# Sums of squares of four RMS norms: eight TensorE products, or three VectorE halvings and one product

## The reference, cut to what is computed

```python
def rms_norm(x, g):
    xf = x.astype(jnp.float32)
    inv = lax.rsqrt(jnp.mean(xf * xf, axis=-1, keepdims=True) + EPS)
    return (xf * inv).astype(x.dtype) * g
...
def modulate(h, shift, scale):
    return h * (1 + scale[:, None, :]) + shift[:, None, :]
...
def ffn_sublayer(x, mod, base, g, w1, w3, w2):
    h = modulate(rms_norm(x, g), mod[:, base], mod[:, base + 1])
    gate = 1 + mod[:, base + 2][:, None, :]
    return x + MACARON_W * gate * swiglu(h, w1, w3, w2)
```

## Time and profile before

| what | us |
|---|---|
| median of 3 runs | 3716.43 |
| lowest and highest run | 3714.55, 3716.44 |
| span of the profiled execution (first to last instruction) | 3719.7 |
| PE busy | 3549.7 |
| DVE busy | 1276.8 |
| ACT busy | 909.3 |
| POOL busy | 705.8 |

### The profile page before, as it was taken

One profiled execution on the slowest core, in us unless ns is written; L12 is line 12 of the kernel. 1 busy time (PEld: TensorE's weight loads), 2 busy tenths in 40 slices (PEclk: granted clock), 3 DMA queues, 4 the chain that ended last, 5 costly groups with the idle time before them and its releaser, 6 DMA issues.

```text
span 3719.7 us, 53696 instructions
## 1 busy us (share of the span) xinstructions
PE 3549.7 (95%) x21007; PEld 3244.3 (87%) x21007; DVE 1276.8 (34%) x2798; ACT 909.3 (24%) x1360; POOL 705.8 (19%) x282
## 2 busy tenths in 40 slices
PE   8889999999999999999998998888999999999997
PEld 2269999999988999999998888444998999999997
DVE  1242322223256232232413766333324232223225
ACT  0031111111134232322323665222013111111112
POOL 0012322232201111111122221000111322223220
PEclk9999999999999999999999999999999999999999
DMA  8721111111111313131443333887510111111101
GB/s 303 240 76 34 45 40 50 34 42 37 57 51 61 106 65 106 48 117 54 151 146 109 89 92 82 276 279 254 194 56 28 35 44 56 34 34 45 50 18 51
DMA packets 245498, 343.11 MB, mean 92 GB/s; under 512 B 56093, under 2 KB 164053, under 8 KB 245138
## 3 DMA queue, kind: packets, MB, share of 16 engines
q1 hardware_dynamic: 218962, 308.42, 25.9%
q10 hardware_dynamic: 26432, 33.18, 2.4%
HBM read 293.54 MB, written 48.01 MB: 92 GB/s over the span
## 4 chain that ended last, share of the span: by engine, by line
PE 89%; DVE 3%; DMA 3%; issue 2%; ACT 2%; SPq 2%; DVEq 0%; ACTq 0%
PE psum L269 24%; PE psum L273 24%; PE psum L272 24%; PE psum L465 4%; PE psum L1412 3%; DMA kn<-k_t 2%; PE psum L1642 2%; PE psum L1392 1%; PE psum L1629 1%; PE psum L990 1%; DVE h_f L612 1%; PE psum L1379 1%; PE psum L1673 1%; PE psum L594 1%; SPq L1596 1%
## 5 line engine op out<-in xcount | busy, mean ns | idle before, releaser
L269 PE MATMUL psum<-acts_hi,w_hi 128*128 128x384 f32 x4032 | 1372.1, 340 | 29.4 <-issue 18.5
L273 PE MATMUL psum<-acts_hi,w_lo 128*128 128x384 f32 x4032 | 1359.8, 337 | 0.0
L272 PE MATMUL psum<-acts_lo,w_hi 128*128 128x384 f32 x4032 | 1359.8, 337 | 0.0
L259 POOL TENSOR_TENSOR w_lo<-w_raw,w_hi 128x2048 fp32r<-128x2048 f32 x106 | 494.1, 4670 | 1821.4 <-ACT w_hi L253 1821.4
L269 PEld LDWEIGHTS psum<-acts_hi,w_hi 128*128 128x128 f32 x4032 | 761.9, 189 | 35.6 <-issue 30.8
L272 PEld LDWEIGHTS psum<-acts_lo,w_hi 128*128 128x128 f32 x4032 | 761.8, 189 | 3.3
L273 PEld LDWEIGHTS psum<-acts_hi,w_lo 128*128 128x128 f32 x4032 | 761.5, 189 | 0.0
L806 DVE TENSOR_TENSOR u_f<-psum,gated 128x384 f32<-128x384 f32 x132 | 73.6, 558 | 994.2 <-ACT gated L761 994.2
L829 DVE SCALAR_TENSOR_TENSOR x<-psum,mods,x 128x384 f32<-128x384 f32 (+1 forms) x552 | 314.9, 570 | 194.6 <-PE psum L273 194.6
L253 ACT ACTIVATE w_hi<-w_raw 128x2048 fp32r<-128x2048 f32 x106 | 200.5, 1910 | 644.4 <-PE psum L269 606.0
L269 PE MATMUL psum<-u_hi,w_hi 128*128 128x384 f32 x1056 | 357.6, 339 | 0.0
(11 more groups left out here) (224 smaller groups left out, 2880.5 us busy)
## 6 DMA issues: line engine op xcount, KB each, us to landing
w_raw<-in_ffn_w SPq DMA_DIRECT2D x66, 1024.0 KB, 5.4
ada_w<-in_w_ada SPq DMA_DIRECT2D x18, 2048.0 KB, 9.6
kc<-in_cache_k SPq DMA_DIRECT2D x16, 2048.0 KB, 10.3
vc<-in_cache_v SPq DMA_DIRECT2D x16, 2048.0 KB, 8.5
w_raw<-in_w_in SPq DMA_DIRECT2D x28, 1024.0 KB, 5.2
sp<-sample_bias SPq DMA_DIRECT2D x128, 65.0 KB, 6.7
ada_w<-in_w_ada_f SPq DMA_DIRECT2D x4, 2048.0 KB, 15.6
kf<-k_t SPq DMA_DIRECT2D x32, 256.0 KB, 4.6
```

The costliest lines, as they stand in the source:

```text
L259: eng.tensor_tensor(w_lo[st][:], w_raw[raw][:], w_hi[st][:].bitcast(F32), ALU.subtract).then_inc(sem("w_lo_done"), 1)
L269: pass1 = eng.matmul(out, whi, ahi, start=first, stop=False)
L272: eng.matmul(out, whi, alo, start=False, stop=False)
L273: return eng.matmul(out, wlo, ahi, start=False, stop=last)
```

## The change

Between the square and the sum stands a new step, `norm_fold`: DVE adds the upper half of the channel blocks of `sq` to the lower half, in place, three times (8 blocks to 4, to 2, to 1), each addition waiting for the one before. `norm_sum` is then one product of the block that is left. The folds are placed by hand in DVE's order: norm 0 all three ahead of `norm_inverse` 0; norms 1 and 3 in the last pass of the FFN, chunk c-1 after the addition of block 3 of chunk c, and chunk 2 after the last addition; norm 2 after the additions of q = 20, q = 22 and q = 23. The last pass of `ffn_vector` is written out. The new semaphore `sq_folded` takes the place of `lf16_turned` and `new_f_ready`, whose increments go to `state_rows_turned` and `lf16_moved`.

```diff
+    FOLDS = 3
+
+    def norm_fold(eng, n, c):
+
+        g = NC * n + c
+        s = sq[:, :, tokens_of(c)]
+        eng.wait_ge(sem("sq_ready"), g + 1)
+        for step in range(FOLDS):
+            half = KT // 2 >> step
+            if step:
+                eng.wait_ge(sem("sq_folded"), FOLDS * g + step)
+            eng.tensor_tensor(s[:, 0:half, :], s[:, 0:half, :], s[:, half:2 * half, :], ALU.add).then_inc(sem("sq_folded"), 1)
+
     def norm_sum(eng, n, c):
 
-        eng.wait_ge(sem("sq_ready"), NC * n + c + 1)
-        for k in range(KT):
-            last = eng.matmul(stats(n, c), ones[:], sq[:, k, tokens_of(c)], start=(k == 0), stop=(k == KT - 1))
-        last.then_inc(sem("ss_ready"), 1)
+        eng.wait_ge(sem("sq_folded"), FOLDS * (NC * n + c + 1))
+        eng.matmul(stats(n, c), ones[:], sq[:, 0, tokens_of(c)], start=True, stop=True).then_inc(sem("ss_ready"), 1)
...
     def norm_vector(eng, n):
+        if n == 0:
+            for c in range(NC):
+                norm_fold(eng, n, c)
         norm_inverse(eng, n, 0)
...
-        def body(i, first_step):
+        def body(i, first_step, last_step=False):
...
                     add_gated(eng, ps[4 + d % 4], x, d, c, gate, "y_free", it * 8 + d + f * KT)
+                    if last_step and c >= 1 and d == 3:
+                        norm_fold(eng, 2 * f + 1, c - 1)
+            if last_step:
+                norm_fold(eng, 2 * f + 1, NC - 1)
 
         body(0, True)
-        with eng.Fori(1, FF_PAIRS) as i:
+        with eng.Fori(1, FF_PAIRS - 1) as i:
             body(i, False)
+        body(FF_PAIRS - 1, False, last_step=True)
...
-        eng.wait_ge(sem("new_f_ready"), 1)
+        eng.wait_ge(sem("lf16_moved"), 2)
...
-                eng.transpose(ps[6][:, 0:ST], lf16[:], ident[0:ST, 0:ST]).then_inc(sem("lf16_turned"), 1)
+                eng.transpose(ps[6][:, 0:ST], lf16[:], ident[0:ST, 0:ST]).then_inc(sem("state_rows_turned"), 1)
...
-                eng.wait_ge(sem("lf16_turned"), 1)
+                eng.wait_ge(sem("state_rows_turned"), 2)
...
-                minus_sums(eng, new_f[:], new_logf[:], past_last[:]).then_inc(sem("new_f_ready"), 1)
+                minus_sums(eng, new_f[:], new_logf[:], past_last[:]).then_inc(sem("lf16_moved"), 1)
...
             add_gated(eng, ps[n], x, d, c, 5, "o_free", FF_PAIRS * KT + d)
+            if q in (20, 22):
+                norm_fold(eng, 2, q // 2 - 10)
+        norm_fold(eng, 2, NC - 1)
```

## The result

| | median us | ratio to before, 95% interval |
|---|---|---|
| kernel before | 3715.5 | 1 |
| changed kernel | 3736.9 | 1.0059 (1.0045 to 1.0074) |

The account below looks back on a forecast made before the run. The prediction took the start of DVE's first reciprocal in each norm as the bound. Its terms, 3.8 + 3.9 + 1.7 + 3.9 = 13.3 us, added to 3716.4 gave 3729.7 us (0.36% slower), range 3722 to 3736.

Parts of the forecast that it names:

- What bounds the kernel: At each norm, the start of DVE's first reciprocal sets the time, not how much PE is spared.
- The four norms: First reciprocals of norms 0 to 3 start later by 3.8, 3.9, 1.7 and 3.9 us.
- DVE becomes the limit of chunk 2: In norm 1, DVE's last additions end 2.3 us earlier than before, not 4.5.
- PE's idle time ahead of `h_lo`: Sign in the changed kernel's trace: this idle time rises from 5 us to over 10 at norms 1 and 2.
- PE's work is the bound: Rival over the whole kernel: sparing PE products makes it faster, 3662 us, or 3689 with six sums counted; chance 0.04.
- swallowed later: Rival: idle time ahead of line 269 absorbs norms 0 and 1's 7.7 us, leaving +5.6, 3722.0 us; chance 0.10.
- PE stalls on the folds: Rival at norms 1 and 3: a late square lets chunk 0's fold hold PE, 6.6 us more, 3736.3; chance 0.08.
- What else: DVE's written-out last FFN pass costs nothing, at most 0.4 us a norm; renamed semaphores cost nothing.
- The clock: At both FFN starts, PE's varying time at its low clock level changes the total by -1.2 to +1.2 us.

Follow-up runs that it names:

- folds_chunks01: The changed kernel with folds for chunks 0 and 1 only, chunk 2 keeping its eight products: 3707.7 us, 0.9972 of the kernel before.
- without_norm1: The changed kernel without its folds in norm 1, which keeps eight products for each sum: 3726.9 us, 1.0035 of the kernel before.
- fold2_behind_scale0: The changed kernel, all twelve folds, with chunk 2's fold moved behind chunk 0's scaling and chunk 0's low part ahead of the second reciprocal: 3717.4 us, 1.0000 of before.
- after_fourth: The changed kernel run a fourth time, unaltered, beside the two norm 1 kernels: 3736.4 us, 1.0059 of the kernel before.
- norm1_alone: The changed kernel with folds in norm 1 only, the other nine sums keeping eight products: 3719.9 us, 1.0012 of the kernel before.
- fold_chunk2: The changed kernel with the fold of chunk 2 only, chunks 0 and 1 keeping their eight products: 3741.0 us, 1.0058 of the kernel before.
- fold_chunk0: The changed kernel with the fold of chunk 0 only, chunks 1 and 2 keeping their eight products: 3702.5 us, 0.9958 of the kernel before.
- peel_only: The changed kernel with no folds, only the last pass written out and the semaphores renamed: 3719.0 us, 1.0013 of the kernel before.

## Why the prediction was right and wrong

**What bounds the kernel: right.** PE's busy time fell by 36 us and the end moved the other way. The reciprocal starts as the fold ends, to 0.1 us by the rows.

**The four norms: right in each term.** Forecast +3.8, +3.9, +1.7, +3.9; read from the stages +3.76, +3.94, +1.72, +3.93. The step inside norm 1 that needed most working, that DVE becomes the limit of chunk 2 and 2.3 us of the sum are gained instead of 4.5, is shown twice: by the packed additions at 1071.90 and 1081.33, and by folds_chunks01 (2.2). PE's idle time ahead of `h_lo` was forecast at over 10 us, and it is 12.6 to 12.7. The rivals "PE's work is the bound" and "swallowed later" are out. "PE stalls on the folds" would have lengthened norms 1 and 3 by 3.3 us each, and they are longer by what the forecast said; that this rival's total of 3736.3 lies next to the measured 3736.9 is chance.

**The step that failed: "What else" and "The clock" as the whole remainder.** I treated all that lies between two norms as a pure shift and gave the clock -1.2 to +1.2 us, at the two FFN starts only. One small term (the start of FFN 2) lay inside that bound; one small and one large were missing.

*The start of FFN 2* was inside its bound. Stretches (columns as in the earlier trace rows), first of before, then of the changed kernel:

```profile
2837.80:2841.80 4.00, 3.98 (x13) 3.99 (x14) 3.96 (x4) 0.92 (x2) 0.00 (x0) 0.51 0.02 4
```

```profile
2852.90:2858.70 5.80, 5.74 (x18) 5.75 (x19) 5.76 (x7) 2.45 (x4) 0.00 (x0) 0.51 0.01 3
3706.00:3709.70 3.70, 3.67 (x16) 3.27 (x16) 3.67 (x2) 0.25 (x1) 0.00 (x0) 0.50 0.02 4
```

13 matmuls at 1.2 GHz have become 18, and FFN 2 is 0.6 us longer in the mean. (The two stretches that I called in agreement with a variation between runs are two starts of one run, and can't show that; the traces of the changed kernel can, at the end of this document.)

*The tail is not a pure shift.* The last stretch above is norm 3's first transposes: 16 of them in 3.67 us at a granted 0.50, behind 6.29 us of idle time. Before, they ran at full clock, as the same two views of that kernel show:

```profile
3687.40 1.91 PE L852 MATMUL psum<-ident,h_f 128*128 128x128 f32 x16
```

```profile
3687.40:3689.40 2.00, 1.91 (x17) 1.67 (x15) 1.97 (x2) 0.56 (x1) 0.00 (x0) 1.00 0.00 0
```

The sums of norm 3 had kept PE at work up to there; one product of two matmuls does not. But these 1.76 us are not what the tail has grown by: without_norm1 has the same transposes behind the same wait at the same clock, and its tail is 41.7 us, as before's.

```profile
3691.40 3.67 PE L880 MATMUL psum<-ident,h_f 128*128 128x128 f32 x16 [6.29 <-DVE h_f L643]
```

```profile
3691.40:3695.10 3.70, 3.67 (x16) 3.27 (x16) 3.67 (x2) 0.24 (x1) 0.00 (x0) 0.50 0.00 0
```

In both kernels, as before, the first output transfer is issued 16.6 us behind the reciprocal. What differs stands at the end: the last two copies of the output, on ACT and on DVE, wait for the same transfer, and in the changed kernel DVE's starts 0.4 us behind ACT's. The timelines, of the changed kernel and then of without_norm1:

```profile
3735.86 0.60 ACT L889 ACTIVATE y_rows<-psum 128x512 f32<-128x512 f32 x1 [0.59 <-DMA out_y_prompt<-y_rows]
3736.24 0.69 DVE L898 COPY y_rows<-psum 128x512 f32<-128x512 f32 x1 [0.87 <-DMA out_y_prompt<-y_rows]
```

```profile
3721.27 0.60 ACT L898 ACTIVATE y_rows<-psum 128x512 f32<-128x512 f32 x1 [0.56 <-DMA out_y_prompt<-y_rows]
3721.28 0.69 DVE L907 COPY y_rows<-psum 128x512 f32<-128x512 f32 x1 [0.47 <-DMA out_y_prompt<-y_rows]
```

The last transfer then takes 3.2 us from issue to landing, in place of 2.6 or 2.7. The same two delays, 0.4 and 0.6 us, stand in all four traces of the changed kernel and in that of fold2_behind_scale0, and in none of the other eight; and in the same five traces, and no other, an 8 KB packet of a queue that the profile calls "instruction" moves during that last transfer. So this goes with all twelve folds in the program and not with norm 3. That the packet is the cause isn't shown.

*The mixer* is the large one, between 5 and 6 us. Prompt attention and sample attention of the changed kernel, first in the trace of the result, then prompt attention in that of after_fourth:

```profile
2000.50:2335.60 335.10, 301.62 (x2302) 285.24 (x2303) 222.51 (x956) 195.51 (x414) 71.07 (x30) 0.94 0.37 94
2335.60:2619.40 283.80, 241.06 (x2224) 135.64 (x2226) 99.15 (x242) 70.36 (x128) 0.00 (x0) 0.93 0.85 265
```

```profile
1999.30:2334.40 335.10, 303.80 (x2301) 288.09 (x2302) 223.10 (x956) 195.81 (x414) 71.18 (x30) 0.92 0.36 94
```

The same two stages of before, and then of norm1_alone:

```profile
1993.00:2321.50 328.50, 293.01 (x2302) 277.33 (x2303) 221.57 (x956) 194.80 (x414) 71.08 (x30) 0.96 0.37 95
2321.50:2606.10 284.60, 241.36 (x2228) 135.33 (x2227) 99.05 (x242) 70.30 (x128) 0.00 (x0) 0.93 0.84 264
```

```profile
1994.60:2326.10 331.50, 297.25 (x2292) 281.02 (x2291) 223.12 (x958) 195.46 (x414) 71.09 (x30) 0.94 0.37 94
2326.10:2600.50 274.40, 233.87 (x2217) 131.62 (x2220) 99.09 (x242) 70.46 (x128) 0.00 (x0) 0.96 0.86 274
```

The work is the same in all (the counts differ by a few records; norm1_alone's stretches lie 1.4 us early), and the length goes roughly with the granted clock: prompt attention 328.5 us at 0.96, 331.5 at 0.94, 335.1 at 0.94 and 0.92; sample attention 274.4 at 0.96, 284.6 at 0.93. What is added stands in PE's busy time and not in its waits: the changed kernel's prompt attention is 6.6 us longer than before's with 8.6 us more of busy time. One and the same work varies by up to 10 us between executions of one kernel (812.9 to 822.8 us for the last three stages of the changed one), and the changed kernel's has on the average more time at the low level: 92, 78, 89 and 106 us in these stages, where the other nine traces have 61 to 89, some 71 in the mean. That this carries the 5 us fits the traces, but no run changed the clock alone. Why these stages should find a lower clock when all twelve folds are there is open. It is not norm 1 by itself (norm1_alone), nor a later arrival (fold_chunk2 arrives 4 us later still, and has no rest), nor the place of chunk 2's fold (fold2_behind_scale0 has 4 us left over too). The written-out pass and the renamed semaphores are also in fold_chunk0, folds_chunks01, fold_chunk2 and norm1_alone, whose means come within 2 us of what their stages add up to; so that code by itself is an unlikely cause, though peel_only's runs don't exclude it. What the two kernels with the rest share is all twelve folds, and the longer program that comes with them, of which the tail's packet may be a sign; that rival was not tested. With one trace for most kernels and a spread of that size, chance has some part in it too.

So the sign, the place and the norms' sum held; the step that failed put everything between the norms at a pure shift, and that came to some 7 us (between 5 and 6 in the mixer, 1.1 in the tail, 0.3 in the two FFNs together). The range was too narrow above, since it had no term for a part of the kernel that the change doesn't touch; what makes the mixer longer stays open.

## What to carry to other kernels

In this kernel a reduction taken off the busy engine pays where that engine's work stood among other work of its own (4.4 us a norm), or where it was on the chain itself and the other engine idle (2.2 us at norm 0); behind the last product the same reduction on the other engine is added to the chain, with whatever it waits for. Before an operation is put in an in-order stream, ask what stands behind it there: the twelve folds cost 20 us with chunk 2's ahead of the first reciprocal, nothing with it behind the scaling of chunk 0, and of the twelve the four of chunk 0, alone, give 15 us (3702.5 us, 0.42% less than before). A range for a kernel of some ms should have room for the spread of the stages between, which one trace of before doesn't show; compare two or more.

## What was not expected of the hardware

PE's granted clock in stages of many short waits differs from one execution to the next (0.93 to 0.96 in sample attention), and 284.6 or 274.4 us go with it, for the same instructions. The transposes of 128 x 128 that a norm's sums had kept at full clock took 3.67 us for 16 at the low level, in place of 1.91, and the end did not move by it (without_norm1). The Trainium skill (page "TensorE: Matmul & The Clock Gate", section "What's actually happening") has the number of slow matmuls at a start vary between runs of one kernel. The traces agree: at FFN 2's start 18 matmuls of the changed kernel begin at 1.2 GHz in three traces, and 12 in the fourth.
